# Gate features beside the whole state-space scan, and the branch projections moved behind it

## The reference

```python
h = rmsnorm(x);  u = h @ w_in          # z | x,B,C | dt | q,k,v | z_att | q_mem | z_mem | gates (3 x 1024)
# A: causal conv(4) + silu on x,B,C, then a scan over chunks of 128 tokens with a carried state
cb = C @ B^T;  y = (cb * exp(acs_l - acs_s)) @ (x*dt) + exp(acs) * (C @ state)
state = state * exp(acs_last) + B^T @ (decay * x*dt)
y_ssd = rmsnorm((y + d_skip * x) * silu(z))          # 16 heads x 64, 4 groups, state 128
# the sample group: the same, each of 8 sequences with its own initial state (16 x 64 x 128)
# B: dilated window attention -> y_att    C: attention into memory -> y_mem
merged = g0 * (y_ssd @ w_br_ssd) + g1 * (y_att @ w_br_att) + g2 * (y_mem @ w_br_mem)   # g = sigmoid(gates)
y = rmsnorm(x + merged @ w_out)
```

## Time and profile before

| | |
|---|---|
| time, three runs | 2384.73, 2397.72, 2397.36 us (median 2397.36) |
| profiled execution | 2396.68 us |
| its span in the trace | 2394.9 us |
| busy share PE / DVE / ACT / POOL | 90% / 45% / 30% / 10% |
| mean granted TensorE clock | 0.93 of full |

### The profile page before, as it was taken

One profiled execution on the slowest core, in us unless ns is written; L12 is line 12 of the kernel. 1 busy time (PEld: TensorE's weight loads), 2 busy tenths in 40 slices (PEclk: granted clock), 3 DMA queues, 4 the chain that ended last, 5 costly groups with the idle time before them and its releaser, 6 DMA issues.

```text
span 2394.9 us, 35765 instructions
## 1 busy us (share of the span) xinstructions
PE 2154.2 (90%) x14762; PEld 1996.3 (83%) x14762; DVE 1066.4 (45%) x2153; ACT 721.0 (30%) x1490; POOL 240.9 (10%) x364
## 2 busy tenths in 40 slices
PE   4899998999699999999988999898999876988997
PEld 4699998989699899999986778338998866987997
DVE  5214665535353534343354882103554554444423
ACT  4223443123423323236441112103343421123202
POOL 1001111000001101112120000001111110000000
PEclk8899999999899999999997989798999977788998
DMA  6211331211011111122353554463333444435422
GB/s 198 73 51 41 104 91 55 77 45 32 28 53 41 58 55 51 62 80 82 133 184 106 178 165 144 135 225 117 98 107 111 139 121 118 142 120 179 152 83 99
DMA packets 166899, 247.59 MB, mean 103 GB/s; under 512 B 19702, under 2 KB 114614, under 8 KB 166710
## 3 DMA queue, kind: packets, MB, share of 16 engines
q1 hardware_dynamic: 144288, 178.91, 24.1%
q0 software_dynamic: 22448, 66.39, 8.5%
HBM read 179.14 MB, written 66.11 MB: 102 GB/s over the span
## 4 chain that ended last, share of the span: by engine, by line
PE 74%; DVE 9%; DMA 6%; issue 5%; ACT 5%; SPq 1%; POOL 0%; DVEq 0%; ACTq 0%; POOLq 0%
PE bank L2102 19%; PE bank L2103 18%; PE bank L2104 18%; PE bank L2269 2%; PE bank L2376 2%; PE bank L2244 2%; PE bank L2227 2%; DVE w_lo L1568 2%; PE bank L2491 1%; ACT w_hi L1273 1%; PE bank L2205 1%; DVE Lm L1993 1%; ACT soft L1398 1%; DMA w_raw<-in_w_in 1%; PE bank L2312 1%
## 5 line engine op out<-in xcount | busy, mean ns | idle before, releaser
L2102 PE MATMUL bank<-w_hi,hT_hi 128*128 128x256 f32 (+1 forms) x2016 | 587.0, 291 | 26.7 <-ACT hT_hi L1381 18.5
L2103 PE MATMUL bank<-w_lo,hT_hi 128*128 128x256 f32 (+1 forms) x2016 | 574.6, 285 | 0.0
L2104 PE MATMUL bank<-w_hi,hT_lo 128*128 128x256 f32 (+1 forms) x2016 | 571.2, 283 | 0.0
L2102 PE MATMUL bank<-hT_hi,w_hi 128*128 128x352 f32 x1344 | 462.1, 344 | 23.5 <-DVE acc L1939 9.7
L2103 PE MATMUL bank<-hT_lo,w_hi 128*128 128x352 f32 x1344 | 446.0, 332 | 0.0
L2104 PE MATMUL bank<-hT_hi,w_lo 128*128 128x352 f32 x1344 | 445.4, 331 | 0.0
L2102 PEld LDWEIGHTS bank<-w_hi,hT_hi 128*128 128x128 f32 (+1 forms) x2016 | 371.3, 184 | 30.2 <-issue 24.0
L2104 PEld LDWEIGHTS bank<-w_hi,hT_lo 128*128 128x128 f32 (+1 forms) x2016 | 371.9, 184 | 1.9
L2103 PEld LDWEIGHTS bank<-w_lo,hT_hi 128*128 128x128 f32 (+1 forms) x2016 | 371.3, 184 | 1.7
L2102 PEld LDWEIGHTS bank<-hT_hi,w_hi 128*128 128x128 f32 x1344 | 265.7, 198 | 38.4 <-issue 12.0
L2103 PEld LDWEIGHTS bank<-hT_lo,w_hi 128*128 128x128 f32 x1344 | 266.4, 198 | 0.5
(11 more groups left out here) (393 smaller groups left out, 3004.9 us busy)
## 6 DMA issues: line engine op xcount, KB each, us to landing
w_raw<-in_w_in SPq DMA_DIRECT2D x96, 512.0 KB, 5.0
kvring<-in_cache_win_kv SPq DMA_DIRECT2D x144, 256.0 KB, 3.4
...
```

The source lines that it names most:

```text
L2102: pe.matmul(out, xh(k), wh(k), start=(k == 0), stop=False)
L2103: pe.matmul(out, xh(k), wl(k), start=False, stop=False)
L2104: ins = pe.matmul(out, xl(k), wh(k), start=False, stop=(k == nk - 1))
```

## The change

Seven gate chunks (45 to 51) lie beside 48 groups of the scan, up to the sample's second sequence; the sample's attention has eight chunks beside it instead of nine. `ya` is done beside sequences 1 to 5 of the sample's scan, its loads (`yal`) apart from its copies. All of `p1` comes behind `("ssd", 8, 6)`, with `yb` dealt between its steps one by one. SP's loads of `xc` for chunk c+1 stand at `("ssd", c, 3)`, of `zt` at `("ssd", c, 4)`, those of old states one or two steps earlier, the first gate pair ahead of `p1`, and `p2`'s first pair ahead of the end of `p1`. `low` steps in the scan go behind the next q=3.

```diff
-N_MEM_FILL, N_TAIL_FILL, N_SAMPLE_FILL = 8, 2, 9
+N_MEM_FILL, N_TAIL_FILL, N_SAMPLE_FILL = 8, 2, 8
...
-    core += [[("ssd", NB, q)] for q in (4, 5, 6)] + [[("yb", 2 * k), ("yb", 2 * k + 1)] for k in range(4)]
-    n_gate, n_ya = 31, 4
+    core += [[("ssd", NB, q)] for q in (4, 5, 6)]
+    n_gate, n_ya = 48, 4
+    core[n_gate - 4] += [("yal", k) for k in range(3)]
+    for i in range(n_ya):
+        core[n_gate + i] += [("yal", k) for k in (3 + i, 7) if k < KT8 and (k < 7 or i == n_ya - 1)]
+        core[n_gate + i] += [("ya", 2 * i), ("ya", 2 * i + 1)]
     sched += spread(core[:n_gate], gate_steps(len(fill_src)))
-    for i in range(n_ya):
-        sched += core[n_gate + i] + [("ya", 2 * i), ("ya", 2 * i + 1)]
+    for x in core[n_gate:]:
+        sched += x
...
-    sched += spread(core[n_gate + n_ya:], steps)
+    sched += spread([[]] * 2 + [[("yb", k)] for k in range(KT8)] + [[]], steps)
...
-        later = [k for k in range(i + 1, min(i + 16, len(sched))) if sched[k][0] == "pv"]
+        later = [k for k in range(i + 1, min(i + 16, len(sched))) if sched[k][0] == "pv" or sched[k][0] == "ssd" and sched[k][2] == 3]
...
         def prev_slot(b):
-            return yst[:, :, :] if b % 2 == 0 else xflat[:, D:2 * D].rearrange("p (i n) -> p i n", i=8)
+            return yst[:, :, :] if b % 2 else xflat[:, D:2 * D].rearrange("p (i n) -> p i n", i=8)
...
         def ya_slot(k):
-            return (yraw[:, :], acc1[:, :], gate1[:, 0, :], gate1[:, 1, :])[k % 4]
+            return (yraw, acc1, acc0)[k % 3][:, :]
...
+        yb_at = (0, 1, 2, 0, 1, 2, 0, 0)
...
-                elif s[0] == "ya":
+                elif s[0] == "yal":
                     k = s[1]
-                    if k == 2:
+                    if k == 0:
+                        late_free(sp)
+                    if k >= 3:
+                        sp.wait_ge(s_yal, k - 2)
+                    sp.dma_start(ya_slot(k), yT[8 + k]).then_inc(s_kv[k % 3], 16)
+                    if k == 7:
                         gates_stored(sp)
-                    if k >= 4:
-                        sp.wait_ge(s_yal, k - 3)
-                    sp.dma_start(ya_slot(k), yT[8 + k]).then_inc(s_kv[k % 4], 16)
+                        for i in range(2):
+                            sp.dma_start(gate1[:, i, :], featT[FT_GATE + 8 * (i + 1)]).then_inc(s_g1, 16)
...
                 elif s[0] == "p1" and s[3] == 0 and s[4] == 0:
                     ft = chunks[s[1]][1] + s[2]
                     if ft == 0:
-                        sp.wait_ge(s_yal, KT8)
-                    else:
-                        sp.wait_ge(s_p1, ft)
+                        continue
+                    sp.wait_ge(s_p1, ft)
                     for i in range(2):
                         sp.dma_start(gate1[:, i, :], featT[FT_GATE + 8 * (i + 1) + ft]).then_inc(s_g1, 16)
...
-                elif s[0] == "ssd" and s[2] == 0:
-                    c = s[1]
+                elif s == ("ssd", 0, 0) or s[0] == "ssd" and s[2] == 3 and s[1] < NB:
+                    c = s[1] + 1 if s[2] else 0
...
-                    if c:
-                        sp.wait_ge(s_dyd, c)
+                        load_prev(0)
+                    if c == 0:
+                        sp.dma_start(zt[:, :], zrow[0:P]).then_inc(s_zt, 16)
+                elif s[0] == "ssd" and s[2] == 4 and s[1] < NB:
+                    c = s[1] + 1
+                    sp.wait_ge(s_dyd, c)
                     m = P if c < NB else NS
                     sp.dma_start(zt[0:m, :], zrow[P * c:P * c + m]).then_inc(s_zt, 16)
-                elif s[0] == "ssd_sb":
-                    b = s[1]
-                    if b == 0:
-                        for i in range(2):
-                            sp.wait_ge(s_yst[i], 16 * 4)
-                    if b >= 2:
-                        sp.wait_ge(s_en, b - 1)
...
+                elif s[0] == "ssd_sb" and s[1] + 2 < BS:
+                    sp.wait_ge(s_en, s[1] + 1)
+                    load_prev(s[1] + 2)
```

More of the change, by code:

```diff
@@ L885, in build_program @@
             gate_no["p2", ft] = n_sig
+        yb_at = (0, 1, 2, 0, 1, 2, 0, 0)
+        acc_use = [sum((f in (0, 2, 4)) == (ft in (0, 2, 4)) for f in range(ft)) for ft in range(KT8)]
+        n_acc = (3, 5)
         def yb_slot(k):
-            return (yraw2, gate2, acc2)[k % 3][:, :]
+            return (yraw2, gate2, acc2)[yb_at[k]][:, :]
         def yst_of(c):
@@ L1035, in _ @@
                             sp.wait_ge(s_yst[i], 16 * (5 - i))
-                    if k >= 3:
-                        sp.wait_ge(s_yal, KT8 + k - 2)
-                    sp.dma_start(yb_slot(k), yT[k]).then_inc(s_kv[k % 3], 16)
+                    if yb_at[k] in yb_at[:k]:
+                        old = max(x for x in range(k) if yb_at[x] == yb_at[k])
+                        sp.wait_ge(s_yal, KT8 + old + 1)
+                    sp.dma_start(yb_slot(k), yT[k]).then_inc(s_kv[yb_at[k]], 16)
                 elif s[0] == "p1" and s[3] == 0 and s[4] == 0:
@@ L1199, in _ @@
                     pool.wait_ge(s_p1, ft + 1)
-                    pool.dma_start(accT[ft], acc_of(ft)[:, :]).then_inc(s_p1st[ft % 2], 16)
+                    pool.dma_start(accT[ft], acc_of(ft)[:, :]).then_inc(s_p1st[ft not in (0, 2, 4)], 16)
                 elif s[0] == "ssd" and s[2] == 0:
@@ L1934, in _ @@
                     if br == 0:
-                        if ft >= 2 and j == 0:
-                            dve.wait_ge(s_p1st[ft % 2], 16 * (ft // 2))
+                        if acc_use[ft] and j == 0:
+                            dve.wait_ge(s_p1st[ft not in (0, 2, 4)], 16 * acc_use[ft])
                         elif j == 0:
```

40 lines of the change are left out of this document (23 added, 17 removed).

## The result

The changed kernel took 2407.83 us (median of 8 runs, 2404.32 to 2417.05), the kernel before 2389.15 us in the 8 runs taken with it. The ratio is 1.0082 with a 95% interval of 1.0056 to 1.0108: slower by 0.8%. I had forecast 2389 us against 2396.68, so 0.3% faster; the time lies inside my range (2354 to 2418), on the other side of no change.

A forecast was written before the change was run, and what follows sets the result against it. Idle time and half-speed matmuls in the last 275 us before `p2` were taken as the loss. Terms to `p2` summed to 531 against 521 us (+10); with -1.8 and -16.5, -8 on 2396.68 gave 2389 us, range 2354 to 2418.

The forecast's parts named there:

- part 1: Sample's attention: six thirds leave, worth 23.5 us of PE time; 16.5 us saved, bounds 8 and 23.5.
- part 2: Prompt chunks 0 to 6 with 30 thirds: 34 us with five thirds, 32 with four, 228 us in all.
- parts 3 and 4: Chunk 7 takes 46 us, with 8.0 not covered; state turn, chunk 8 and sequence 0 take 31.5 us.
- part 5: Sample's scan without cover, sequence 1 to the last rows: 90 us, most later sequences 9.3 each; bounds 72 and 100.
- part 6: `p1` alone: 131 us, tiles 2 to 7 at 17.2 us each from gate reload stalls and half-clock matmuls.
- `p2` on: `yb` and the start of `p2`: 1.8 us saved, as `p2`'s first pair is issued ahead and it starts at full speed.
- The chain of 31.5 us: Prompt chunks: 25.2 us to the `xc` issue, 5.8 landing and half a us; decides with four thirds, where PE needs 29.8.
- unit cost: Prompt chunks 0 to 5 before: 39.3 us each, 23.4 of thirds and 15.9 of the scan's own matmuls and waits.
- 131 and not 121: `p1` alone: 131 us with the clock falling in its stalls, 121 without the fall; the slow clock was taken.
- Slower by the gate pair: `p1`'s gate pair lands 10 us after issue instead of 6.5, seven tiles cost 24.5 us more: 2413 us, chance 0.13.
- The interleaving rule: Advises interleaving regimes with different busiest engines; taking `p1` out of the sample's scan puts the result on the slower side, 0.13.
- The scan did shorten: Rival it judges: prompt chunks stay at 38 to 39 us though thirds leave, +35, 2424 us, chance 0.05.

The follow-up runs named there:

- a_fill9: Changed kernel with nine feature chunks beside the sample's attention instead of eight, so 36 thirds beside the scan instead of 42: 2411.60 us, ratio 1.0105 to the kernel before.
- mid44_7: mid44 with seven feature chunks beside the sample's attention and 48 thirds in the scan: 2372.78 us, ratio 0.9937 to the kernel before.
- mid44: h_yb_tail with the 42 gate thirds beside 44 groups instead of 48 and `p1` from sequence 2 on: 2363.02 us, ratio 0.9900 to the kernel before.
- a_tail: Changed kernel with `p1` begun beside the sample's sequences 5 to 7 and the last rows: 2389.72 us, ratio 0.9999 to the kernel before.
- h_yb_tail: Changed kernel with gate buffers reloaded apart, `y_s` loads one group earlier, `p1` begun beside sample's sequences 5 to 7 and last rows: 2370.35 us, ratio 0.9912.

## Why the prediction failed

By its own terms, in us, predicted and then read from the trace after:

| term | predicted | measured |
|---|---|---|
| part 1, the sample's attention | -16.5 | -6.1 |
| part 2, chunks 0 to 6 | 228 | 235.5 |
| parts 3 and 4, chunk 7 to sequence 0 | 77.5 (a third left out) | 80.1 |
| part 5, bare sample's scan | 90 | 85.9 |
| part 6, `p1` alone | 131 | 137.9 |
| `p2` on | -1.8 | -1.2 |

**The steps that failed are the sizes of part 1, part 2 and part 6,** by 10.4, 7.5 and 6.9 us, all to the same side. Parts 1 and 2 have one mistake in common: I took time off for thirds that leave, and in these stages waits grew in their place. In part 6 the mechanism is in the trace, and its size was short.

**Part 1 failed most**, and outside its bound of 8. By stages, four `z` steps gave 8.2 us between the first merge and the first window key (112.0 to 103.8), near the 9 that I took. The window keys, where I took 4 for two thirds, took 148.6 us in both kernels. From the first memory key to the scan, where I took 3.5 for one third, it got 2.1 longer (222.6 to 224.7). The windows of the window keys, before and after, and of the last of these stretches in the kernel after:

```profile
1289.60:1438.20 148.60, 137.39 (x602) 108.59 (x602) 128.51 (x194) 19.86 (x42) 3.21 (x6) 0.85 0.51 158
1274.40:1423.00 148.60, 130.96 (x578) 100.94 (x577) 126.32 (x193) 18.31 (x37) 4.84 (x9) 0.84 0.53 163
1423.00:1647.70 224.70, 195.40 (x916) 130.72 (x917) 33.28 (x69) 38.78 (x85) 9.23 (x17) 0.90 0.49 156
```

PE is idle in them anyway (17.6 and 29.3 us after), at a clock of 0.84 and 0.90: a removed third leaves a gap. From the first merge to the scan PE's busy time fell by 20.5 us and its idle time rose by 14.4. Two waits that grew, in the kernel after and then in a_fill9, which puts the thirds back:

```profile
PE bank L2315 <- DMA vS<-qkv_sample: 10.8, 1, 10.8
PE bank L2366 <- DVE srow L1859: 9.3, 2, 5.9
...
PE bank L2315 <- DMA vS<-qkv_sample: 7.9, 1, 7.9
PE bank L2366 <- DVE srow L1859: 6.7, 2, 3.3
```

a_fill9 lost 4.5 us in this stretch. One more chunk, taken out in mid44_7, gave 14.9 against mid44; why so much more than the first was not looked into.

**Part 2** was 7.5 short. The chain of 31.5 us that I read from chunk 5 was not what holds a chunk with four thirds: these took 33.8 on average (30.4 to 35.6), as much as those with five (33.3). I had priced PE and chain as two separate bounds and taken the larger; in fact a group without a third exposes its own wait (3.3 us on the state, 3.1 on `Lm`) while the others are full, and slow matmuls follow. The windows of chunks 3 and 4 and a_fill9 show it. Besides, my unit cost had a slip: by the order, chunks 0 to 5 of the kernel before hold 35 thirds and not 36, so a chunk's own part was 16.5 us and not 15.9.

**Part 6** had the mechanism (a pair that lands in 6.2 us at the median, stalls of 4 us, slow matmuls behind) and missed 4 us in pitch (17.9 for 17.2 in six tiles) and 3 in its first tiles and last. What it missed is that this is a cost of the order of loads, which two small edits take down by 24 us. It was right to set 131 and not 121: the 108.4 us busy for 93.7 of work show the low clock behind the stalls, and it fell behind stalls of 2.7 us already, where I had put the least at 4.15. The rule that I leaned on there does not reach this loop. The Trainium skill, TensorE: Matmul & The Clock Gate, section on HAM oscillation, speaks of a loop whose compute is shorter than its DMA wait; here a tile has 11.7 us of work and a stall of 2.7 to 5.7. The clock fell all the same, so the number stands on the rows and not on that rule.

**Parts 3, 4 and 5** held, with some luck: the wait for `xtok` was 4.2 us plus a slow step, `xc` of chunk 8 had no wait, later sequences took 9.0 for 9.3. But from the state turn to sequence 0 the order has six thirds, and I counted five; my sum holds 41 of the 42. With the missing 3.9 us parts 3 and 4 come to 81.4, and the forecast to 2393.

**The rivals.** "Slower by the gate pair" gave 2413 by a landing of 10 us; the landing was 6.2 and the time came out near it (2407.83) by luck, for other reasons. The interleaving rule of the Trainium skill (Perfetto Trace Analysis, section Optimization Strategy) pointed to the right side: a_tail and h_yb_tail, which put `p1` back beside the sample's scan, gained 18 and 14 us. I named it, and gave its side 0.13. The scan did shorten (chunks of 33.6 us with 30 thirds in seven, for 39.3 with 35 in six), so that rival is out.

**The base.** I summed against one execution of 2396.68 us, and before's 8 runs have a median of 2389.15. The stages before the first merge, where nothing changed, moved by 7 us between the two traces. A forecast of -8 is within what two single executions differ by. From the median, my -8 would have been 2381, 27 us under the result. And I had taken 24 us as what can be told from no change; with eight runs of each kernel the interval is 6 us to either side.

In short: the change took out the waits that it aimed at, but nearly the same amount came back, at the bare gate reload of `p1` and in the bare sample's scan. h_yb_tail shows both at once: with the reload split and `p1` begun earlier, the same 42 thirds and all of `p1` take 497.5 us from the scan to `p2` instead of 539.4, and the kernel is 0.9% faster than before.
